# State-space input table multiplied together in its turned layout, from tables of powers and of B loaded from memory; no transposes of it in the blocks

## The reference, cut to what matters

```python
dt = exp(log_dt); a = exp(lam * dt)               # 2 directions, 64 groups, 64 states, complex
q = (a - 1) / lam;  bb = q * b                    # 16 inputs per group
s[t, g, p] = sum_h u[t, g, h] * bb[g, p, h]
x[t] = a * x[t - 1] + s[t]                        # forward, and backward for direction 1
y[t, g, h] = re(sum_p x[t, g, p] * c[g, h, p])    # both directions added
```

## Time and profile before

| | us |
|---|---|
| three runs | 2054.59, 2057.17, 2057.46 (median 2057.17) |
| profiled execution, its own time | 2054.32 |
| its span, first to last instruction | 2052.5 |
| TensorE busy | 2008.0 |
| VectorE busy | 1085.8 |
| ScalarE busy | 594.9 |
| mean granted TensorE clock | 0.997 of full |

### The profile page before, as it was taken

The page is one execution under the profiler, slowest core; times in us unless marked ns, Lnnn a source line. Parts: engine busy times, 40 slices in busy tenths (PEclk is TensorE's granted clock), DMA queues, the critical chain, the costliest instruction groups (busy, mean ns, idle before and its releaser), DMA issues.

```text
span 2052.5 us, 26821 instructions
## 1 busy us (share of the span) xinstructions
PE 2008.0 (98%) x10086; PEld 1640.1 (80%) x10086; DVE 1085.8 (53%) x1640; ACT 594.9 (29%) x845; POOL 27.4 (1%) x16
## 2 busy tenths in 40 slices
PE   4999999999999999999999999999999999999998
PEld 1568888888888888888888888888888888888886
DVE  4545799999998645554433434332433333333325
ACT  5325343334343322222222222222322222222222
POOL 0003100000000000000000000000000000000000
PEclk9999999999999999999999999999999999999999
DMA  9963544344344544443334444443233333334423
GB/s 361 366 199 116 168 106 109 102 106 108 102 108 112 179 129 133 125 138 108 100 94 138 134 123 138 133 133 104 73 92 102 93 97 97 93 101 154 173 99 128
DMA packets 384079, 270.72 MB, mean 132 GB/s; under 512 B 24820, under 2 KB 349916, under 8 KB 382164
## 3 DMA queue, kind: packets, MB, share of 16 engines
q1 hardware_dynamic: 373728, 265.61, 42.0%
q10 hardware_dynamic: 10292, 4.33, 1.5%
HBM read 251.81 MB, written 18.09 MB: 131 GB/s over the span
## 4 chain that ended last, share of the span: by engine, by line
PE 93%; DVE 3%; ACT 2%; DMA 1%; issue 1%; SPq 0%; ACTq 0%; DVEq 0%
PE ac L753 25%; PE ac L757 25%; PE ac L754 24%; PE ac L938 1%; PE ac L939 1%; PE ac L937 1%; PE ss L815 1%; PE ss L586 1%; PE ss L939 1%; PE ss L938 1%; PE ss L937 1%; PE ac L633 1%; PE ac L634 1%; PE ac L637 1%; DMA wslot<-w_in 1%; PE ss L808 1%
## 5 line engine op out<-in xcount | busy, mean ns | idle before, releaser
L1557 DVE TENSOR_TENSOR wlo<-wslot,whi 128x1024 fp32r<-128x1024 f32 x309 | 378.3, 1224 | 643.4 <-ACT whi L973 639.3
L973 ACT ACTIVATE whi<-wslot 128x1024 fp32r<-128x1024 f32 x327 | 346.9, 1061 | 1244.3 <-PE ac L757 1042.8
L753 PE MATMUL ac<-hxh,whi 128*128 128x512 f32 x1664 | 651.9, 392 | 0.0
L754 PE MATMUL ac<-hxl,whi 128*128 128x512 f32 x1664 | 647.8, 389 | 0.0
L757 PE MATMUL ac<-hxh,wlo 128*128 128x512 f32 x1664 | 411.2, 389 | 0.9 <-DVE wlo L1557 0.9
L753 PEld LDWEIGHTS ac<-hxh,whi 128*128 128x128 f32 x1664 | 312.4, 188 | 67.4 <-issue 2.9
L757 PEld LDWEIGHTS ac<-hxh,wlo 128*128 128x128 f32 x1664 | 312.3, 188 | 66.1 <-DVE wlo L1557 1.3
L754 PEld LDWEIGHTS ac<-hxl,whi 128*128 128x128 f32 x1664 | 312.4, 188 | 63.8
L753 PE MATMUL ac<-bah,whi 128*128 128x512 f32 x384 | 149.4, 389 | 0.0
L754 PE MATMUL ac<-bal,whi 128*128 128x512 f32 x384 | 149.4, 389 | 0.0
L757 PE MATMUL ac<-bah,wlo 128*128 128x512 f32 x384 | 94.8, 389 | 0.0
(11 more groups left out here) (359 smaller groups left out, 2076.0 us busy)
## 6 DMA issues: line engine op xcount, KB each, us to landing
wslot<-w_in SPq DMA_DIRECT2D x224, 512.0 KB, 3.8
ring<-w_ada SPq DMA_DIRECT2D x64, 512.0 KB, 8.4
gwt<-w_ada SPq DMA_DIRECT2D x128, 128.0 KB, 2.5
wslot<-w_out SPq DMA_DIRECT2D x32, 512.0 KB, 3.6
wslot<-proj_a SPq DMA_DIRECT2D x16, 512.0 KB, 4.1
wslot<-proj_b SPq DMA_DIRECT2D x16, 512.0 KB, 4.1
wslot<-proj_c SPq DMA_DIRECT2D x16, 512.0 KB, 3.9
xn<-x SPq DMA_DIRECT2D x4, 1024.0 KB, 9.6
```

The costliest lines, as they stand in the source:

```text
L753: mm(ac[:, bank, :], w, xh, start=(v == 0 and q == 0), stop=False)
L754: mm(ac[:, bank, :], w, xl, start=False, stop=False)
L973: cp = lambda o, i, scale=1.0: nc.scalar.activation(o, i, ACT.Copy, scale=scale)
L1557: tt(wlo[:, s, :], wslot[:, s, :], whi[:, (U0[k] + j) % 2, :].bitcast(F32), ALU.subtract)\
```

## The change

V is no longer made with states on partitions and then turned. Its two factors are brought in the turned layout (8 places x 16 inputs on the 128 partitions, groups and states on the free axis): Ah holds the powers of a, the same for the 16 inputs of a place; Bh holds B, the same for the 8 places. VectorE multiplies them straight into VT. The taps need B alone and take it from the table tile. The factors lie in two new DRAM tensors written ahead of the first block: `bh_dram` from Bn (q times b, now made by VectorE before TensorE's transposes for the old table), `ah_dram` from An (eight powers). ScalarE's swapped copy of B goes away, as do VT's copies and the tile B2. Buffers are placed anew. Ah and Bh are loaded for each block in four DMAs, two behind weight load 1 and two behind weight load 2 of the block ahead, and `tab_load` moves behind load 7.

```diff
+        def state_tables(b, parts):
+            for d in parts:
+                for side, dst, src in ((0, Ah, ah_dram), (1, Bh, bh_dram)):
...
+                    if not isinstance(b, int) or b:
+                        sp.wait_ge(v_done, b)
+                    rows_ = src[:, d].rearrange("n g c -> n (g c)")[:, bass.ds(b * (GB * 2 * P), GB * 2 * P)]
+                    if side == 0:
+                        rows_ = rows_.unsqueeze(1).to_broadcast([L, H, GB * 2 * P])
+                    else:
+                        rows_ = rows_.unsqueeze(0).to_broadcast([L, H, GB * 2 * P])
+                    sp.dma_start(dst[:, d * GB:(d + 1) * GB, :, :].rearrange("p g r q -> p (g r q)"), rows_)\
+                        .then_inc(vt_in, 16)
...
-                    if k == 1 and j == 5 and not (isinstance(i, int) and i == NB - 1):
+                    if k == 1 and j in (1, 2) and not (isinstance(i, int) and i == NB - 1):
+                        state_tables(i + 1, (j - 1,))
+                    if k == 1 and j == 7 and not (isinstance(i, int) and i == NB - 1):
                         tab_load(i + 1)
...
         def conv_turn(b):
             product(1, b, 0, 2, 0, xs_of, mid=None if first else (lambda: y_back(b)))
+            product(1, b, 2, 2, 1, xs_of)
+            pe.wait_ge(u_in, b * (16 * L) + 16 * L)
             pe.wait_ge(v_done, b + 1)
             for d in range(2):
                 if d and not first:
                     pe.wait_ge(yb_cp, b)
-                for g in range(GB):
-                    last = tr(ss[:, 2 * d + g // 4, (g % 4) * 128:(g % 4 + 1) * 128], V[:, d, g, :], ident[:, :])
-                last.then_inc(vt_ps, 1)
-            product(1, b, 2, 2, 1, xs_of)
...
-                                  V[:, d, g, at0:at0 + H], Cp[:, d, g, cp0:cp0 + L * H], start=True, stop=True)
+                                  tB1[:, d * GB + g, :], Cp[:, d, g, cp0:cp0 + L * H], start=True, stop=True)
...
+        tt(Bn[:, :, 0, :], qr, br, ALU.mult)
+        tt(Bn[:, :, 1, :], qr, bi, ALU.mult)
+        link(tt(btmp[:, :, :], qi, bi, ALU.mult))
+        link(tt(Bn[:, :, 0, :], Bn[:, :, 0, :], btmp[:, :, :], ALU.subtract))
+        link(tt(btmp[:, :, :], qi, br, ALU.mult))
+        tt(Bn[:, :, 1, :], Bn[:, :, 1, :], btmp[:, :, :], ALU.add).then_inc(bb_done, 1)
...
-        tt(Brw2[:, :, :], Brw2[:, :, :], qb(1), ALU.mult)
-        link(tt(B1[:, :, :], B1[:, :, :], qb(0), ALU.mult))
-        tt(B1[:, :, :], B1[:, :, :], Brw2[:, :, :], ALU.add).then_inc(bb_done, 1)
...
         def state_mults(b):
-            dve.wait_ge(bc2, b + 1)
...
-            for d in range(2):
...
-                last, o = powers(V[:, d], (tAr, tAi), 0, L, d == 0, b, d, tB1[:, d * 8:d * 8 + 8, :],
-                                 B2[:, d], tmp)
+            dve.wait_ge(vt_in, b * 64 + 64)
+            ar, ai = (Ah[:, :, ri, :].unsqueeze(2).to_broadcast([128, 2 * GB, 2, P]) for ri in range(2))
+            tt(VT4, ar, Bh[:, :, :, :], ALU.mult)
+            link(tt(t_v, ai, Bh[:, :, ::-1, :], ALU.mult))
         def state_adds():
...
+            tt(VT4[:, :, 0, :], VT4[:, :, 0, :], t_v[:, :, 0, :], ALU.subtract)
+            tt(VT4[:, :, 1, :], VT4[:, :, 1, :], t_v[:, :, 1, :], ALU.add).then_inc(v_done, 1)
```

More of the change, by code:

```diff
@@ L155, in program @@
     Abr = r("Abr", [128, KW * T])
-    PWr = r("PWr", [128, 7, 64])
-    PWi = r("PWi", [128, 7, 64])
     R8 = r("R8", [128, 64])
@@ L478, in _ @@
         tab_load(0)
+        state_tables(0, range(2))
         sp.wait_ge(u_out[0], 16)
@@ L676, in p0_c @@
             pe.wait_ge(p0_cp, 2)
+            pe.wait_ge(b_in, 64)
             for h in range(H):
@@ L1132, in conv_turn @@
             cp(xas[:, :], ac[:, 0, :]).then_inc(ac_free[0], 1)
+            hi(1, b, 4)
+            hi(1, b, 5)
             if not first:
                 act.wait_ge(x_done, b)
[L1135 to L1141 removed]
             for d in range(2):
@@ L1534, in _ @@
             link(ts_(PWi[:, n + 1, :], pw1[:, :], 2.0, None, ALU.mult))
-        dve.wait_ge(brw_done, 1)
-        qb = lambda n: q2[:, n, :].unsqueeze(2).to_broadcast([128, 128, H])
-        tt(Brw2[:, :, :], Brw2[:, :, :], qb(1), ALU.mult)
-        link(tt(B1[:, :, :], B1[:, :, :], qb(0), ALU.mult))
-        tt(B1[:, :, :], B1[:, :, :], Brw2[:, :, :], ALU.add).then_inc(bb_done, 1)
+        v.memset(An[:, 0, 0, :], 1.0)
+        v.memset(An[:, 0, 1, :], 0.0)
+        cpy(An[:, 1, 0, :], z(0))
+        link(cpy(An[:, 1, 1, :], z(1)))
+        for n0, m in ((1, 1), (2, 2), (4, 3)):
+            mr, mi = (An[:, n0:n0 + 1, ri, :].to_broadcast([128, m, P]) for ri in range(2))
+            sr, si = (An[:, 1:1 + m, ri, :] for ri in range(2))
+            dr, di = (An[:, n0 + 1:n0 + 1 + m, ri, :] for ri in range(2))
+            ta, tb = (btmp[:, 4 * q:4 * q + m, :] for q in range(2))
+            tt(dr, sr, mr, ALU.mult)
+            tt(di, sr, mi, ALU.mult)
+            tt(ta, si, mi, ALU.mult)
+            link(tt(tb, si, mr, ALU.mult))
+            tt(dr, dr, ta, ALU.subtract)
+            last = tt(di, di, tb, ALU.add)
+            if m < 3:
+                link(last)
+        last.then_inc(an_done, 1)
         def powers(dst, A, e0, n, rev, b, d, T1, T2, tmp):
```

115 lines of the change are left out of this document (56 added, 59 removed).

## The result

| | before | after |
|---|---|---|
| median of four runs, us | 2057.32 | 2143.42 |
| lowest to highest | 2054.59 to 2059.25 | 2142.36 to 2151.74 |
| profiled execution: its span | 2052.5 | 2149.7 |
| mean granted TensorE clock | 0.997 | 0.976 |

The ratio is 1.0432 (95% interval 1.0417 to 1.0447): 86 us slower, where +12.5 was forecast. The direction was right, the size wrong by a factor of seven. The other three executions of after were 8 to 9.4 us shorter than this one; no trace of them is kept, so where those 8 us stand is open.

The account below looks back on a forecast made before the run. TensorE bounds the kernel, by 2.9 us in 54.4. Ahead of the blocks +8.4, block 0 -1.9 and -1.3, six rounds +9.9, last block -1.9, less 0.7: +12.5 us, 2069.7 against the median. Predicted 2069.5, range 2045 to 2084.

Parts of the forecast that it names:

- The transposes: In each block, TensorE's 16 transposes lie on the path; dropping them saves 1.9 us a block, 15.2 us over eight.
- VectorE's own work: Table products and sums in each block: cost taken as 0, bounds -0.3 and +2.4 us; VectorE's loop 51.6 us.
- The wait and the place: In SyncE's queue, weight loads 2 and 3 leave after v_done and tables; VectorE 4.5 us late, period 56.1 us, +9.9 us.
- The failed step: Ah and Bh loads in each block: 8 engines at 25.5 GB/s each, 2.57 us a table; with 16 engines 1.22.
- the prediction's own formula: In each block, weight load 3 lands 2.0 + 4 tables + 2 x 1.64 us after v_done, forecast 15.6 us.
- Rival A: Table loads use all 16 engines, nothing waits in the blocks, 52.5 us a block: -13.5 us, 2043.7; chance 14%.
- Rival C: Rereading rows is slower (3.5 us a table, 2095) or VectorE's products take the 2.4 us bound (another 14 us); chance 10%.
- The head: Ahead of the first block: +1.7 us at unit 6 and a 6.7 us stall for load 7, together +8.4 us.
- The stall of unit 7: Ahead of the blocks, load 7 stands behind four tables (10.3 us) and U (1.5); TensorE stalls 6.7 us.
- The C chain: Ahead of the blocks, An's 0.5 MB delays the B store, ScalarE's C copies, C store and load 6: +1.7 us.
- Bn's end: Ahead of the first block, VectorE ends Bn by about 168.5, before TensorE transposes it at 169.28: cost 0 to 2 us.

Follow-up runs that it names:

- experiment 4: Changed kernel with table loads of blocks 1 to 7 cut to 64 bytes of each row, waits and order kept: 2060.79 us.
- experiment 5: Changed kernel with the next block's table loads put behind weight loads 4 and 6, still 8 outer rows: 2062.7 us.
- experiment 6: Kernel of experiment 1 (16 outer rows) with the table loads put behind weight loads 4 and 6: 2055.37 us.
- experiment 7: Experiment 6 with u stores and loads of units 4 to 7 ahead of waits, U ahead of the first block's tables: 2045.06 us.
- experiment 1: Changed kernel with partitions permuted so that the table sources' slowest dimension is 16 instead of 8: 2075.2 us, ratio 1.0097.
- experiment 12: Changed kernel with each table load cut into four of 8 x 4 rows of x, to 32 neighbouring partitions: 2112.55 us.
- experiment 13: Same four loads of 8 x 4 rows as experiment 12, each to 32 partitions four apart: 2107.57 us.
- experiment 3: Changed kernel with table loads reading 128 consecutive rows of x, slowest dimension 128: 2058.18 us.
- experiment 17: Changed kernel with one 16 x 8 load a table, reading 128 neighbouring rows of x, each group backwards: 2078.03 us.
- experiment 18: Experiment 3 with every third row of x in place of neighbouring rows: 2060.43 us.
- experiment 2: Changed kernel with table loads reading 8 x 16 different rows of x, each read once: 2143.38 us.
- experiment 9: Changed kernel with table loads reading 16 x 8 different rows of x, each read once: 2078.45 us.
- experiment 8: Experiment 6 with four of the six operations that make Bn cut to one sixteenth: 2050.38 us.
- experiment 10: Changed kernel with each table load cut into eight of 16 rows, to 16 neighbouring partitions: 2113.42 us.
- experiment 11: Same eight loads of 16 rows as experiment 10, each to partitions eight apart, U and M permuted to match: 2162.03 us.
- experiment 14: Changed kernel with each table load cut into 16 of eight rows of x, to eight neighbouring partitions: 2169.92 us.
- experiment 15: Same 16 loads of eight rows as experiment 14, each to eight partitions four apart: 2335.51 us.
- experiment 16: Same 16 loads of eight rows as experiment 14, each to eight partitions 16 apart: 2304.84 us.

## Why the prediction was wrong, step by step

**The transposes: right.** Periods without the tables' trouble are 52.65 in experiments 4 to 7 and in the last block: 1.8 us under 54.44, with 1.9 forecast.

**VectorE's own work: right.** Less its waits of over 0.2 us, a period is 51.3 us in the changed kernel (67.66 - 16.3) and 51.2 in experiment 1 (55.7 - 4.5), where 51.6 was taken: the products and sums cost 0.3 to 0.4 us less than before, at the low bound of the prediction.

**The wait and the place: right in kind.** The queue held the weight loads back behind v_done and the tables, VectorE was late at units 2 and 3, and its loop set the period. Two details were wrong: VectorE was late at unit 2 as well, and its wait ahead of Z did not go (0.8 to 1.4 us). In all six periods together VectorE waits 84.7 us ahead of the low parts of units 2 and 3 and 8.6 us ahead of cv and Z.

**The failed step: "By analogy 8 engines carry them, at 204 GB/s: 2.57 us for each 512 KB."** The number of engines was inferred well; the share with the tables nearly alone is 0.51, and experiment 1 halves the time with 16. The rate of one engine was taken from one row, a copy from memory to memory, and was up to twice what loads of this shape get: 5.1 us a table measured by the prediction's own formula, 3.9 by the rate of 133 GB/s in the window, and by the formula 2.6 with 16 engines. (The formula's 1.64 us for a weight load stands in no row shown, and the weight loads shared these engines, so part of the 5.1 may be theirs.) Experiments 12 and 13 show single packets at the rate that was taken; experiments 3, 17 and 18 that one load of 16 x 8 rows doesn't get it and one of 128 rows comes near it (344 GB/s over 16 engines, 21.5 each). Rival A fell with the same figure: it priced 16 engines at 1.22 us and -13.5 us in all, and they give +19. The size follows from the prediction's own chain. Load 3 is ready at 25.6 + 1.06 in place of 16.8, VectorE is 14.5 us late in place of 4.5, keeps waits of 0.8 to 2.1 us ahead of cv and Z, and six rounds cost 74 us in place of 10. A threshold lies in front of this term (12.3 us of slack), so an error of 2 in the rate became one of 3 in the delay and, after the 2.9 us that VectorE had to spare, of 7 in the sum. Rival C held that case, but for a reason that was wrong (rereading, rejected by experiments 2 and 9), and capped at 3.5 us a table; the range ended at 2084.

**The head: mis-sized the same way.** Forecast for the first readout was 8.4 - 3.2 = +5.2, measured +24.7 (24.85 from the copy of Ar). The differences between runs, all from the copy of Ar, divide it in this order: the first block's slow loads for block 1, 6.9 (changed kernel less experiment 5); 8 engines in place of 16, 8.4 (experiment 5 less 6); the queue's order, 8.7 (6 less 7); what is left, 0.75 (7 less before). The stall of unit 7 was named, but with 10.3 us of tables at the wrong rate, and the U loads behind them were counted at 1.5 us where they took 10.32 only to be issued. The C chain was +6.9 us late at the store, not +1.7: Ar came 11 us later behind Bn, whose sixth operation ended at 171.7 and not at 168.5, and u stores and load 4 stood behind its wait in the queue. That delay was not in the sum at all. Bn's end had a cost of 0 to 2 us on TensorE in the prediction; the wait was 2.40, and by experiments 7 and 8 what it is worth depends on the queue behind it.

**The clock.** It was no term of the sum. In the changed kernel TensorE stood idle for 6.53 us ahead of 395.94, and its granted clock was 0.50, the 1.2 GHz level, from 392 and still when it worked again:

```profile
396.00:398.00 2.00, 2.00 (x5) 1.61 (x6) 2.00 (x2) 0.37 (x1) 0.00 (x0) 0.50 0.60 127
398.00:400.00 2.00, 2.00 (x9) 1.59 (x8) 1.68 (x2) 0.00 (x0) 0.00 (x0) 0.79 0.62 142
```

Five matmuls in 2 us where the next window has nine. It happens again at unit 3, and there it reaches the period. The windows below start where unit 3 starts, in the period of 67.66 us and in one of 66.10:

```profile
407.00:415.00 8.00, 8.00 (x24) 6.36 (x25) 7.83 (x9) 1.44 (x2) 0.00 (x0) 0.66 0.77 202
542.00:550.00 8.00, 8.00 (x32) 6.58 (x33) 7.83 (x9) 2.11 (x3) 0.00 (x0) 0.79 0.83 206
```

In the first VectorE waits 0.39 us for TensorE ahead of cv and 1.43 ahead of Z, in the second not at all ahead of cv and 0.91 ahead of Z. The six periods divide so. In the three of 67.06 to 67.93 us such a window has a clock of 0.63 to 0.66 and the two waits make 1.8 to 2.1 us; in the three of 65.65 to 66.43 us it has 0.79 to 0.83, and they make 0.8 to 0.9. So by these rows the slower clock at unit 3 is worth some 1.1 us in each of three periods, a small part of the 74.2.

**What stays open.** Why one load of 8 x 16 or 16 x 8 rows gets so much less out of each engine than one of 128 rows. Rereading and the rows' places in memory are excluded by experiments 2, 9, 17 and 18, and the number of engines alone by experiments 1 and 9, where all 16 are as slow as the eight. Two dimensions of rows by themselves are not the cause either: experiments 10 and 11 have one and are slow, 12 and 13 have two and their packets are fast. The shape also sets which partitions are written together. The Trainium skill, "SBUF — State Buffer", "Door 1", has a map of 16 ports at some 27 GB/s each; by it the forms of 8 x 16, 16 x 8 and 128 rows use 4, 8 and 16 ports at a time if their engines run in step, and from that an estimate of 4.8, 2.4 and 1.2 us a table follows. The first two are near the 5.1 and 2.6 of the formula; with 128 rows the formula gives 2.0, the window of experiment 3 (344 GB/s) 1.5. By the same estimate experiment 1 would halve the time through its ports, whatever its engines do, so their count and the partitions that they write are not told apart by it. Against the map stand the 133 GB/s of the changed kernel, over the 109 of four such ports, and experiments 13 to 16, made to show such collisions in small loads, which show none. So the map fits the order of the large loads and is not shown as their cause. Not tried was one load of 512 KB in which engines and partitions are changed one without the other.

## What to carry to other kernels

When a change puts bulk loads in a queue that weights share, price them by a row of the same shape and the same two ends (one load of 8 x 16 rows ran at well under half the rate of one of 128 rows), and if there is none, carry the rate's error through the slack that follows: here a factor of two in a rate was a factor of seven in the time. Ask first where in the queue the bytes stand: put behind weight loads 4 and 6 the slowest form cost a period nothing (52.65 us), ahead of loads 2 and 3, which VectorE wants 9 and 12 us after v_done, it cost 13 us a block or more. And with one queue in order, put every load that is already free to go ahead of the waits for things still being made; that alone gave 8.7 us by the traces (10 by the medians) and turned no gain into 0.55%.

## What the runs showed of the hardware that was not expected

- The same 512 KB, by the shape of the load: 5.1 us with 8 x 16 rows, 2.6 with 16 x 8, and, by the same formula, about 2.0 with 128 (load 3 was ready 13.1 us after v_done), and for 16 x 8 and 128 rows wherever the rows lay.
- Issuing is not free when the engines are behind: eight U loads of 48 KB took 16.02 us to issue in the changed kernel, 9.09 in experiment 1, 6.67 in experiment 3 and 3.85 in experiment 5, where no tables stand right ahead of them.
- VectorE's operations can last far longer than their size says while GpSimd works on its low parts. In experiment 8 an operation cut to 64 elements took 2.50 us, where others of that size take 0.23:

```profile
164.27 2.50 DVE L1538 TENSOR_TENSOR btmp<-ZN,braw 128x64 f32<-128x64 f32 x1
...
169.45 0.23 DVE L1541 TENSOR_TENSOR Bn<-Bn,btmp 128x64 f32<-128x64 f32 x1
```

  GpSimd's two low parts lie over the first of these rows:

```profile
162.64 6.39 POOL L600 TENSOR_TENSOR wlo<-wslot,whi 128x1024 fp32r<-128x1024 f32 x2 [161.17 <-ACT whi L1008]
```

  The Trainium skill, "SBUF — State Buffer", section "SBUF: two separate sides", says that the two share a pair of ports under an exclusive lock, held for a whole instruction. The trace agrees in kind: with a sixteenth of the work the operation was no shorter (2.50 us, and 2.01 at full size in the changed kernel), and the first operation that began after 169.03, when GpSimd was done, took 0.27.
